# A modulation total placed two blocks later, and another order of copies and weight blocks in the pooling stage of a fused two-block network

## What is computed

```python
# layer 0: attention mixer; layer 1: pooling mixer (i = layer)
sh1, sc1, g1, sh2, sc2, g2 = split(silu(c) @ w_mod[i] + b_mod[i], 6)
y = mixer(x * (1 + sc1) + sh1)                 # layer 1: windowed means minus x, then 4 grouped products
x = layer_norm(ALPHA * x + g1 * y, ln_g[i, 0], ln_b[i, 0])
h = x * (1 + sc2) + sh2
x = layer_norm(ALPHA * x + g2 * ((silu(h @ w_g) * (h @ w_u)) @ w_out), ln_g[i, 1], ln_b[i, 1])
# then a second block on x: rms norm, w_in of 8208 columns, gated linear attention and block attention,
# w_branch_a, w_branch_b, w_out, an MLP of 4096, and a gate
```

## Time and profile before

| | |
|---|---|
| median of 3 runs | 1170.72 us (1170.25 to 1171.26) |
| profiled execution, its own time | 1171.16 us |
| span of its trace | 1169.4 us |
| busy: PE / DVE / ACT | 1132.1 / 769.3 / 567.3 us |
| mean granted TensorE clock | 0.986 of full |
| HBM read, mean rate | 234.75 MB, 202 GB/s |

### The profile page before, as it was taken

The page is one execution under the profiler, slowest core; times in us unless marked ns, Lnnn a source line. Parts: engine busy times, 40 slices in busy tenths (PEclk is TensorE's granted clock), DMA queues, the critical chain, the costliest instruction groups (busy, mean ns, idle before and its releaser), DMA issues.

```text
span 1169.4 us, 15342 instructions
## 1 busy us (share of the span) xinstructions
PE 1132.1 (97%) x6322; PEld 953.2 (82%) x6322; DVE 769.3 (66%) x877; ACT 567.3 (49%) x779; POOL 61.9 (5%) x119
## 2 busy tenths in 40 slices
PE   5999999999999798999999999999999999999998
PEld 3787767799998686999988777876888889998886
DVE  1697498788696889885553864446667667664454
ACT  2642366464444233644442667444855356563342
POOL 0011130001110101000000000010000000000000
PEclk8999999999999897999999999999999999999999
DMA  9986550779897765685554797766633446555540
GB/s 329 381 274 238 198 176 21 249 245 314 303 329 255 284 230 195 212 291 171 183 185 137 163 228 166 173 144 144 147 142 126 163 144 217 182 181 193 195 158 36
DMA packets 120391, 236.80 MB, mean 202 GB/s; under 512 B 5633, under 2 KB 61250, under 8 KB 120194
## 3 DMA queue, kind: packets, MB, share of 16 engines
q1 hardware_dynamic: 105984, 185.48, 51.6%
q0 software_dynamic: 14048, 50.09, 12.2%
q10 hardware_dynamic: 290, 0.26, 0.1%
HBM read 234.75 MB, written 1.05 MB: 202 GB/s over the span
## 4 chain that ended last, share of the span: by engine, by line
PE 89%; DVE 5%; ACT 3%; DMA 2%; issue 2%; SPq 0%; DVEq 0%; ACTq 0%
PE ps L1849 18%; PE ps L1851 18%; PE ps L1850 18%; PE ps L1892 8%; PE ps L1891 8%; PE ps L1890 8%; PE ps L1989 2%; DVE wL L1055 1%; PE ps L2111 1%; PE ps L2150 1%; DVE g2b L1139 1%; PE ps L2039 1%; ACT tf L622 1%; ACT wH L590 1%; DMA mod<-in_w_mod 1%
## 5 line engine op out<-in xcount | busy, mean ns | idle before, releaser
L1055 DVE TENSOR_TENSOR wL<-raw,wH 128x1024 fp32r<-128x1024 f32 x328 | 397.4, 1222 | 239.2 <-ACT wH L590 238.2
L590 ACT ACTIVATE wH<-raw 128x1024 fp32r<-128x1024 f32 x328 | 342.8, 1057 | 392.7 <-PE ps L1851 248.0
L1849 PE MATMUL ps<-wH,aH 128*128 128x512 f32 (+1 forms) x592 | 237.1, 401 | 11.2 <-DVE aL L1067 3.4
L1851 PE MATMUL ps<-wH,aL 128*128 128x512 f32 (+1 forms) x592 | 231.9, 392 | 0.0
L1850 PE MATMUL ps<-wL,aH 128*128 128x512 f32 (+1 forms) x592 | 231.8, 392 | 0.0
L1890 PE MATMUL ps<-aH,wH 128*128 128x256 f32 x768 | 219.4, 286 | 0.0
L1892 PE MATMUL ps<-aH,wL 128*128 128x256 f32 x768 | 217.3, 283 | 0.0
L1891 PE MATMUL ps<-aL,wH 128*128 128x256 f32 x768 | 217.3, 283 | 0.0
L1849 PEld LDWEIGHTS ps<-wH,aH 128*128 128x128 f32 x592 | 113.2, 191 | 43.3 <-issue 13.1
L1890 PEld LDWEIGHTS ps<-aH,wH 128*128 128x128 f32 x768 | 147.4, 192 | 1.0 <-issue 1.0
L1891 PEld LDWEIGHTS ps<-aL,wH 128*128 128x128 f32 x768 | 147.4, 192 | 1.0 <-issue 1.0
(11 more groups left out here) (309 smaller groups left out, 1260.3 us busy)
## 6 DMA issues: line engine op xcount, KB each, us to landing
raw<-in_ffn_w_in SPq DMA_DIRECT2D x88, 512.0 KB
modraw<-in_w_mod POOLq DMA_DIRECT2D x80, 512.0 KB, 6.6
raw<-in_w_in SPq DMA_DIRECT2D x32, 1024.0 KB
raw<-in_ffn_w_out SPq DMA_DIRECT2D x22, 1024.0 KB
raw<-in_w_up SPq DMA_DIRECT2D x16, 1024.0 KB
raw<-in_w_down SPq DMA_DIRECT2D x16, 1024.0 KB
mod<-in_w_mod SPq DMA_DIRECT2D x8, 1024.0 KB, 11.8
raw<-in_attn_w_qkv SPq DMA_DIRECT2D x8, 1024.0 KB
```

The costliest lines, as they stand in the source:

```text
L590: nc.scalar.activation(wH[:, n % WS, :], raw[:, (n // 2) % RAW, (n % 2) * 1024:(n % 2) * 1024 + 1024], ACT.Copy).then_inc(w_hi, 1)
L1055: V.tensor_tensor(wL[:, n % WL, :], raw[:, (n // 2) % RAW, (n % 2) * 1024:(n % 2) * 1024 + 1024], wH[:, n % WS, :].bitcast(fp32), ALU.subt ...
L1849: T.matmul(outp, xh, h, start=first, stop=False)
L1851: return T.matmul(outp, xl, h, start=False, stop=last_)
```

## The change

- The total of vector 7 is taken behind block k = 12 of `out0` (before: k = 10), and DVE puts it behind its loop, ahead of the last modulation step (before: in iteration 12).
- In the pooling stage ACT copies the four banks ahead of the last two weight sub-blocks (before: behind), and at the entry that follows ACT makes the first two activation tiles ahead of two weight sub-blocks.
- On DVE in the pooling stage, the first half of `affine` of tile 0 moves into `residual(1)`, between its two column halves; the four `low` follow each other ahead of `vec_put(8)`; the column vectors `lncol_of(1)` move behind `hat(0)`.
- The total of vector 8 goes to bank 0 (before 2), waits for both tiles of `residual` (before for tile 0), and TensorE waits for its put only ahead of row tile 1 of the grouped product (before ahead of tile 0).
- At the entries `ln(0)` and `ln(3)`, DVE takes the product (L1357) between the two low parts of tile 0, and writes the fifth weight block behind the residual's sum L1362 (before: low part, low part, weight block, product).
- The total of vector 2 in attention: blocks 0 to 2 behind round 14, 3 to 5 behind round 15, 6 and 7 behind the transposes of `o` (before: 0 to 3 behind round 15, 4 to 7 behind the transposes).

```diff
-TOTAL_BANK = {1: 4, 2: 2, 8: 2}
+TOTAL_BANK = {1: 4, 2: 2, 8: 0}
...
-                for j in range(sd_at, 4 if k != 2 else 2):
+                for j in range(sd_at, 4 if k != 2 else 0):
                     adv(n + j)
                 act.wait_ge(lncol_ready, min(norm, 1) + 1)
                 for j in range(2):
                     hi_t(name, j, norm=norm)
-                if k != 2:
-                    for j in range(4, 8):
-                        adv(n + j)
+                for j in range(4, 8) if k != 2 else range(2):
+                    adv(n + j)
...
-            for j in range(6, 8):
-                adv(n + j)
             for j in range(4):
                 act.wait_ge(t_done, GROUPS["pool"] + j + 1)
                 nc.scalar.activation(aH[:, 2 * j:2 * j + 2, :], pbank(j)...)
+            for j in range(6, 8):
+                adv(n + j)
...
                     if t == 1:
-                        for j in range(2):
-                            lo_t(name, j, norm=norm)
-                        adv(subs.pop(0))
+                        lo_t(name, 0, norm=norm)
                     product_done(stage, t)
                     V.tensor_tensor(lnt, pair(un + t), gate_...)
+                    if t == 1:
+                        lo_t(name, 1, norm=norm)
...
                     link(V.scalar_tensor_tensor(out=x[:, t, :], in0=x[:, t, :], scalar=ALPHA, ...))
+                    if t == 1:
+                        adv(subs.pop(0))
...
                         if (t, b) == (0, 0):
                             for j in range(2):
                                 adv(first + j)
+                        elif (t, b) == (1, 0):
+                            dve.wait_ge(pool_h, 1)
+                            affine(0, 0)
...
-                for j in range(2):
+                for j in range(4):
                     low(j)
                 vec_put(IN_FF0 - 1)
-                dve.wait_ge(mod_out, NMOD0 + IN_FF0)
-                lncol_of(1).then_inc(lncol_ready, 1)
-                for j in range(2, 4):
-                    low(j)
-                dve.wait_ge(pool_h, 1)
-                affine(0, 0)
                 affine(0, 1)
                 dve.wait_ge(ln_x, TT + 1)
                 pooled(0)
                 spread(0)
                 rstd(2, 0)
                 hat(0)
+                dve.wait_ge(mod_out, NMOD0 + IN_FF0)
+                lncol_of(1).then_inc(lncol_ready, 1)
...
                         if k == 7:
                             vec_put(6)
-                        elif k == 12:
-                            vec_put(7)
                         vec_steps(1)
...
                 if layer == 0:
+                    vec_put(7)
                     vec_steps(1)
...
-            vec_total(IN_QKV - 1, range(0, 4))
+                if r >= 14:
+                    vec_total(IN_QKV - 1, range(3 * (r - 14), 3 * (r - 13)))
...
-            vec_total(IN_QKV - 1, range(4, KT))
+            vec_total(IN_QKV - 1, range(6, KT))
...
-                    if layer == 0 and k in (5, 10):
-                        vec_total({5: 6, 10: 7}[k])
+                    if layer == 0 and k in (5, 12):
+                        vec_total({5: 6, 12: 7}[k])
...
                 if t == 0:
-                    pe.wait_ge(acc_out, UNITS["out0"] + 1)
+                    pe.wait_ge(acc_out, UNITS["out0"] + 2)
                     vec_total(IN_FF0 - 1)
             n, un = SUBS["pool"], UNITS["pool"]
-            pe.wait_ge(mod_out, NMOD0 + IN_FF0)
             for t in range(TT):
+                if t == 1:
+                    pe.wait_ge(mod_out, NMOD0 + IN_FF0)
```

More of the change, by code:

```diff
@@ L1389, in ln_pool, with affine @@
                 un, first = UNITS["out0"], SUBS["pool"]
+                def affine(t, j):
+                    if j == 0:
+                        V.scalar_tensor_tensor(out=x[:, t, :], in0=x[:, t, :], scalar=mv[:, t, 0:1], in1=lnp[:, 0, :],
+                                               op0=ALU.subtract, op1=ALU.mult).then_inc(ln_hat, 1)
+                    else:
+                        dve.wait_ge(ln_hat, TT + 2 * t + 1)
+                        V.scalar_tensor_tensor(out=x[:, t, :], in0=x[:, t, :], scalar=stat[:, 54 + t:55 + t], in1=lnp[:, 1, :],
+                                               op0=ALU.mult, op1=ALU.add).then_inc(ln_x, 1)
                 def residual(t):
@@ L1450, in low @@
                                     aH[:, 2 * j:2 * j + 2, :].bitcast(fp32), ALU.subtract).then_inc(t_lo, 1)
[L1452 to L1459, removed]
                 def hat(t):
```

## The result

| | before | changed |
|---|---|---|
| median, 4 runs each | 1170.93 us (1170.25 to 1171.26) | 1163.3 us (1162.93 to 1164.57) |
| profiled execution: own time / span | 1171.16 / 1169.4 us | 1163.34 / 1161.6 us |
| mean granted clock | 0.986 | 0.991 |

The ratio is 0.9934, 95% interval 0.9922 to 0.9947: 7.6 us faster, 6.2 to 9.1. The forecast was 1163.7 us, faster. The places of the gain are nearly those of the forecast; the causes are so only in part.

The account below looks back on a forecast made before the run. TensorE, busy 97%, was taken as the bound, with DVE next as the limit. Pooling stage 4.2, entries 2.8 and attention 0 gave 7.0 us off 1171.16: 1164.2, as a median 1163.7 us, range 1160.7 to 1167.3 (8 in 10).

Parts of the forecast that it names:

- DVE as the limit: From the put of vector 6 to the pooling stage, only DVE's four gaps can be won: 2.9 us.
- TensorE's saving passes whole: Rival: TensorE's 9.3 us in `out0` come through undiminished, 14.1 us in all, 1156.6 us; chance 0.06.
- TensorE's wait 1.1 us and the total 1.92 us: In `out0`, the wait ahead of vector 7's total falls from 6.52 to some 0.9 us, the total from 3.55 to 1.84.
- The clock should survive so short a wait: In `out0`, full clock after the short wait: the total saves 1.7 us, the slow matmuls behind it 2.0 us.
- The late load: Last tile of vector 8, used near 414.9, may come late: cost 0.3 us, bounds 0 and 1.4.
- `affine` in `residual(1)`: Pooling stage, DVE: moving the first half costs 0.2 us there and saves 1.3 at its old place, net 1.1 us.
- the copies: Pooling stage: ACT's copies ahead of its weight blocks let DVE's four low parts finish 0.9 us earlier.
- The low clock in the pooling stage: DVE's four low parts end 0.5 us earlier if the clock is low there, 1.3 us if full.
- the clock takes a part back: Rival: 1.2 GHz through the grouped product and the entry's first 30 matmuls, about 3 us lost, 1166.7 us; chance 0.15.
- The entries: At the two entries, TensorE's waits for the sixth weight block go: 1.4 us each, 2.8 us together.
- Attention: Moving pieces of vector 2's total gains 0, bounds -0.2 and 0.4, as the product behind waits for a low part.
- Bank 0 and the total of vector 8: Pooling stage: the total's later wait for the second half of `residual(1)` costs 0, bounds 0 and 0.5 us.

Follow-up runs that it names:

- less_dve: The changed kernel without two DVE instructions of 1.22 us between the put of vector 6 and the pooling stage (output lacks two factors): 1162.56 us, ratio 0.9927.
- affine_back: The changed kernel with the first half of `affine` of tile 0 put back ahead of the second half: 1164.29 us, ratio 0.9939.
- copies_behind: The changed kernel with ACT's four bank copies put back behind its two weight blocks: 1164.16 us, ratio 0.9941.
- no_pool: The kernel before with only the moved total of vector 7 and the new DVE order at the two entries: 1163.92 us, ratio 0.9939.
- total_alone: The kernel before with only the total of vector 7 behind block 12 and its put behind DVE's loop: 1166.91 us, ratio 0.9964.
- both_early: The changed kernel with the total of vector 6 behind block 1 (was 5) and of vector 7 behind block 10 (was 12): 1154.89 us, ratio 0.9864.
- total_k14: The changed kernel with the total of vector 7 behind block 14 (was 12): 1167.64 us, ratio 0.9969.
- sixth_early: The changed kernel with the total of vector 6 behind block 1 (was 5), that of vector 7 left behind block 12: 1161.66 us, ratio 0.992.
- early_9: The changed kernel with the total of vector 6 behind block 1 (was 5) and of vector 7 behind block 9 (was 12): 1155.85 us, ratio 0.9869.

## Why the prediction was right, and where not

**DVE as the limit: right.** The other reading, that TensorE's saving passes whole (1156.6), fell. Gained up to `residual(0)`: 3.35 us, forecast 2.9. All four gaps went; each was worth about 0.09 us more than its idle figure, as DVE's back-to-back rows overlap by that much in the trace (407.05 + 1.27 is 408.32, the next starts at 408.24), which makes 0.35 of the missing 0.45.

**TensorE's wait 1.1 us and the total 1.92 us: right** (0.9 and 1.84). **"The clock should survive so short a wait" was wrong:** it fell right behind the total, for 3.4 us. I had judged by a wait of 1.42 us that had dense matmuls on both sides; here the thin total stands behind the wait. It cost nothing, as DVE waits nowhere for TensorE in this stretch. Dense matmuls then brought it back; the rule of the Trainium skill, TensorE: Matmul & The Clock Gate, section Part 1: The HAM clock gate, that activity releases the throttle, agrees with the row at 402.73.

**The late load: did not come** (forecast 0.3). It is asked for at 413.09 and there, 6.8 us after its issue at 406.29, though the DMA engines were full in between (a share of 1.03 over 406 to 413). less_dve shows how little slack there is. From what the Trainium skill says (DMA: Bandwidth & Descriptors, section Issuing engines are not separate DMA queues), that transfers of all issuers share the same 16 engines, I had derived a load 1.4 us late. The sharing is not refuted; the delay that I drew from it did not come.

**`affine` in `residual(1)`, 1.1 us, and the copies, 0.9 us: the steps that failed.** The trace shows about that gain behind `residual(0)` (4.81 - 3.35 = 1.5 us), but affine_back, copies_behind and no_pool show that neither edit earns it, and total_alone, with neither, gains 1.6 us between the same two rows (28.30 to 26.70). I took the gaps of 1.05 and 1.16 us in the earlier trace rows as things that the reorder removes. Both came from one cause, TensorE and its weight loads being 6 us late, and the moved total had removed it already. I had even written that the product is then done long before, and still counted the removal of `affine` from its old place as 1.3 us: on this full list the instruction costs the same in both places. The pooling stage came to 4.9 us with 4.2 forecast.

**The low clock in the pooling stage was there, as before** (0.50 over 442 to 446 before, 0.50 over 435 to 439 now), and I had put its price at 0.8 us (0.5 against 1.3); the changed kernel against both_early makes it 1.2 us. The rival "the clock takes a part back" named the right place with the wrong size: nothing of it lasted beyond the entry.

**The entries: right in kind, a little small,** 1.5 each for 1.4, and 3.1 us alone. **Attention: right,** 0: the total's pieces fit into TensorE's wait (0.75 down to 0.18 us), and the product behind still waits. **Bank 0 and the total of vector 8:** the total now waits 1.54 us ahead of itself, beside DVE's work: 0, as forecast.

The near hit of the sum, 7.0 for 7.6, is thus in part luck. It has two errors that cancel: 1.1 + 0.9 - 0.45 = 1.55 us credited to edits that do nothing once the total has moved, and a moved total, worth 4.3 us by total_alone, priced at 2.9 - 0.3 = 2.6. With 4.3 for the total and 3.1 for the entries the sum is 7.4, and no_pool, which has just these two, measures 7.5.

## What to carry to other kernels

Before adding up the gaps that several edits remove, ask of each gap who was late, and why: gaps with one cause go with the first edit that removes the cause, and the others then earn nothing. When the late engine has been helped and a second is the limit, walk back along that second engine to its last long wait. Here DVE stood 12.8 us ahead of its full stretch, for loads behind a total that could be taken four blocks sooner; with the next total two blocks sooner as well, that was worth more than the whole change (with the next one left at block 12, only 1.6 us).

## What was not expected of the hardware

- The granted clock fell to the lower level (1.2 GHz) after waits of 1.10, 1.13 and 1.07 us followed by a total of 16 matmuls of 128x2 (the changed kernel, total_alone, no_pool), and for copies_behind and affine_back after only 0.64 and 0.69 us; each time for 3 to 4 us. In copies_behind the first slow matmul (401.55) came over 1 us after dense matmuls had begun again (400.30). In less_dve, with a wait of 0.83 us, it fell during the total itself (2.40 us in place of 1.92) and stayed low for about 6 us. Where the same total followed dense matmuls without a wait (both_early, total_k14, sixth_early, early_9), it stayed at full.
- The waits alone do not settle it. In the kernel before, the pooling matmuls with waits of 0.60 and 0.26 us ahead of them (439.37, 440.82) ended at a granted clock of 0.50 (442 to 444); in both_early the same matmuls with waits of 0.64 and 0.26 us (427.29, 428.74) kept 1.00. What decides between the two, no run here shows.
- The same fall in the pooling stage costs something on the path: the four low parts start 0.91 us apart there, and at the full clock, in both_early, they take 2.73 us together (428.69 to 431.42), in place of 3.41 (436.40 to 439.81). With the later first one it is 1.2 us in all.
- Closing a gap between two DVE rows gave more than its idle figure, as back-to-back rows start up to 0.09 us before the one ahead has ended. The gap of 0.17 us in the earlier trace rows was worth 0.27: from 406.91 to 408.37 it is 1.46 us, and from 407.05 to 408.24 in the changed kernel, without the gap, 1.19.
